# A transformer layer on one core: sums' first group prepared during the dots' last chunks, norms with few TensorE products

## The reference

```python
h = rms_norm(x, norm1_w) * (1 + sc1) + sh1
mix, ... = token_mixer(h, ...)       # attention, SSM
#   in it: y = rms_norm(y.reshape(b, L, SSM_GROUPS, gsz), ...)      2 groups
#          merged = sigmoid(ga) * (o_attn @ w_br_attn) + sigmoid(gs) * (y @ w_br_ssm)
#          mix = merged @ w_out
x = x + g1 * mix
h = rms_norm(x, norm2_w) * (1 + sc2) + sh2
x = x + g2 * peer(h, ...)
y = rms_norm(x, norm_f_w)
# peer: 16384 experts, 8 heads, top 16 of each
act = gelu(einsum('thkd,td->thk', peer_u[e], xb))
out = einsum('thk,thkd->td', g * act, peer_v[e])
```

## Time and profile before

| | us |
|---|---|
| median of 3 runs (lowest to highest) | 4533.72 (4526.81 to 4534.49) |
| time of the profiled execution | 4537.59 |
| its span | 4535.9 |
| busy PE | 4253.7 (94%) |
| busy DVE | 3162.1 (70%) |
| busy ACT | 1418.8 (31%) |
| busy POOL | 983.3 (22%) |

### The profile page before, as it was taken

How to read it: one execution, slowest core, us unless ns; L and a number is a source line. 1 busy time by engine, 2 the same in 40 slices (tenths; PEclk the granted TensorE clock), 3 DMA queues, 4 the chain that set the end, 5 groups by cost and what they waited for, 6 DMA issues and landing times. The chain is left out here.

```text
span 4535.9 us, 67898 instructions
## 1 busy us (share of the span) xinstructions
PE 4253.7 (94%) x24256; PEld 2498.9 (55%) x24256; DVE 3162.1 (70%) x5616; ACT 1418.8 (31%) x1943; POOL 983.3 (22%) x1020
## 2 busy tenths in 40 slices
PE   6999997999988899799999999999969999999997
PEld 3665663444455566466555556655635555555554
DVE  4347335455586534555889888988868888988985
ACT  3333421333321112321334444444432222222221
POOL 0000013322200001100142222222234333333320
PEclk8999998999997899999999999999989999999998
DMA  6752766555354677644586777677789888888881
GB/s 226 242 196 102 237 212 213 150 149 151 117 161 134 243 243 261 226 135 139 179 283 246 277 263 286 253 268 275 269 296 339 290 303 288 303 296 289 304 281 40
DMA packets 422568, 1039.54 MB, mean 229 GB/s; under 512 B 38498, under 2 KB 209122, under 8 KB 413730
## 3 DMA queue, kind: packets, MB, share of 16 engines
q0 software_dynamic: 112896, 396.43, 27.1%
q1 hardware_dynamic: 251970, 403.51, 25.7%
q10 hardware_dynamic: 57440, 236.35, 13.7%
HBM read 809.88 MB, written 226.27 MB: 228 GB/s over the span
## 5 line engine op out<-in xcount | busy, mean ns | idle before, releaser
L455 PE MATMUL dot_ps<-h_parts,u_parts 128*128 128x416 f16 x6144 | 1117.0, 340 | 6.8 <-issue 6.8
L455 PE MATMUL totals_ps<-act_parts,v_parts 128*128 128x416 f16 x6144 | 1083.2, 339 | 42.3 <-DVE act_parts L3219 42.3
L455 PEld LDWEIGHTS totals_ps<-act_parts,v_parts 128*128 128x128 f16 x6144 | 601.6, 98 | 522.6 <-issue 44.8
L455 PEld LDWEIGHTS dot_ps<-h_parts,u_parts 128*128 128x128 f16 x6144 | 594.9, 98 | 461.7 <-issue 14.4
L468 PE MATMUL in_ps<-h_parts_in,in_parts 128*128 128x384 f16 (+1 forms) x3168 | 515.6, 319 | 4.5 <-DVE in_parts L826 4.5
L3294 POOL DMA_INDIRECT rows_in<-in_v,row_v x204 | 302.8, 1484 | 497.7 <-DVE h L3238 484.9
L468 PEld LDWEIGHTS in_ps<-h_parts_in,in_parts 128*128 128x128 f16 x3168 | 311.0, 98 | 171.2 <-DVE in_parts L826 4.6
L2572 POOL DMA_INDIRECT u_rows_in<-tmp_u_rows,row_u x192 | 251.0, 1307 | 586.5 <-DVE row_dot L2914 558.3
L3158 ACT ACTIVATE v_parts<-v_group,units 128x1024 f16<-128x1024 f32 x128 | 136.9, 1138 | 766.8 <-PE totals_ps L455 738.1
L2674 ACT ACTIVATE gelu<-dot_ps,units 128x416 f32<-128x416 f32 x256 | 155.6, 608 | 629.4 <-PE dot_ps L455 614.9
L3230 DVE SCALAR_TENSOR_TENSOR h<-totals_ps,sum_unit,h 128x416 f32<-128x416 f32 x388 | 247.9, 647 | 139.9 <-PE totals_ps L455 139.3
(11 more groups left out here) (402 smaller groups left out, 5899.4 us busy)
## 6 DMA issues: line engine op xcount, KB each, us to landing
u_chunks<-in_u SPq DMA_DIRECT2D x128, 512.0 KB, 6.2
v_group<-in_v SPq DMA_DIRECT2D x31, 2048.0 KB, 8.3
tmp_g<-gelu ACTq DMA_DIRECT2D x128, 416.0 KB, 5.3
tmp_w<-h ACTq DMA_DIRECT2D x26, 2048.0 KB, 10.3
w_groups<-tmp_w SPq DMA_DIRECT2D x32, 1664.0 KB, 11.6
gelu_in<-tmp_g SPq DMA_DIRECT2D x31, 1664.0 KB, 7.5
tmp_u_rows<-proj_rows ACTq DMA_DIRECT2D x64, 512.0 KB, 5.4
attend_v_sweep<-in_v ACTq DMA_DIRECT2D x64, 512.0 KB, 4.3
```

What stands on the lines that cost most here:

```text
L455: mm = pe.matmul(bank, left(x), right(y), start=first and x == 0 and y == 0, stop=last and x == 1)
```

## The change

It has five parts. (1) `Norm`: DVE adds the squares of all chunks to one, and PE multiplies only that with the ones matrix, three products a norm. (2) Merge phase: the group norms' products stand behind the first branch step's 12 products with o; norm2's squares and additions stand inside the mix steps, whose loops on ACT and DVE are written out. (3) Dots phase: weight products and one-hots of the last eight chunks are earlier, 14 rows are moved out of them (2 to the first 16 chunks, 2 to each of the six turns), and in the last chunks SP loads, and ACT, DVE split, the first group of v, w and gelu, into buffers that the dots give up (the second half of the score buffer, one-hot, candidate and u buffers). (4) Sums phase: it starts with group 1's loads; the first group is only counted as done, behind the clearing of the accumulator. (5) The last norm becomes part of the sums phase: DVE gates 832 columns a chunk after each result of the last group and the 256 others in one piece (`gated_rows`), ACT squares, POOL adds chunks 0 to 4 and PE multiplies that sum and chunks 5 to 7 (12 products).

```diff
+    def add(self, dve, k):
+        dve.wait_ge(self.squared, k + 1)
+        if k > 1:
+            dve.wait_ge(self.added, k - 1)
+        total = self.sq[:, 0, :]
+        dve.tensor_tensor(total, total, self.sq[:, k, :], ALU.add).then_inc(self.added, 1)
...
         ones = self.s["const"][:, C_ONE:C_ONE + P]
-        for k in range(self.chunks):
-            pe.wait_ge(self.squared, k + 1)
-            for i, (t0, n) in enumerate(SPLITS):
-                mm = pe.matmul(self.psum[:, i, 0:n], ones, self.sq[:, k, t0:t0 + n],
-                               start=(k == 0), stop=(k == self.chunks - 1))
-                if k == self.chunks - 1:
-                    mm.then_inc(self.summed, 1)
+        pe.wait_ge(self.added, self.chunks - 1)
+        for i, (t0, n) in enumerate(SPLITS):
+            pe.matmul(self.psum[:, i, 0:n], ones, self.sq[:, 0, t0:t0 + n], start=True,
+                      stop=True).then_inc(self.summed, 1)
     def vector(self, dve):
+        for k in range(1, self.chunks):
+            self.add(dve, k)
+        self.means(dve)
...
-                group[0].tensor(pe)
-                group[1].tensor(pe)
+                def branch(i, u, norms=False):
+                    pe.wait_ge(br_in[u], (i + 1) * 64)
...
+                        pe.wait_ge(banks_taken, i * (2 * NS) + u * NS + j + 1)
+                        for k in range(NA):
+                            pe.matmul(ps[:, j, 0:n], wa[:, u, k, :], o[:, k, t0:t0 + n],
+                                      start=(k == 0), stop=(k == NA - 1))
+                        if not norms or j < 2:
+                            turn_fill(i * 2 + u, j)
+                    if norms:
+                        group[0].tensor(pe)
+                        pe.wait_ge(group[0].meaned, NS)
+                        group[1].tensor(pe)
+                        turn_fill(0, 2)
+                    if u == 0:
+                        pe.wait_ge(y_ready, KC)
...
+                for m in range(KC):
+                    for at in range(PASS * Turned.FILLS):
+                        to_rows.scalar(act, KC + m, PASS, at // Turned.FILLS, at % Turned.FILLS, SWEPT)
+                        if m > 0 and at == 4:
+                            act.wait_ge(mix_taken, m + 2)
+                            norm.square(act, m - 1)
...
+                    if m > 1:
+                        norm.add(dve, m - 1)
...
             slot = x * ND + q
-            return [n for n in range(WG // 2) if 4 + n * 11 // (WG // 2) == slot]
+            return [n for n in range(WG // 2) if 3 + n * 9 // (WG // 2) == slot]
...
-        ONEHOT_LAST = {1: 0, 2: 1, 3: 2, 5: 3}
+        ONEHOT_LAST = {1: 0, 2: 1, 3: 2, 4: 3}
         DENSE = TILES - 1
-        ROWS_FIRST = (3, 2, 2, 2, 2, 2, 3, 3, 2, 3, 3, 3, 3, 3, 3, 3)
-        ROWS_TURN = (3, 1, 2, 1, 1, 2, 2, 3, 1, 3, 2, 2, 1, 1, 3, 3)
-        ROWS_TAIL = (4, 3, 3, 3, 4, 3, 4, 4)
+        ROWS_FIRST = (3, 2, 2, 2, 2, 3, 3, 3, 3, 3, 3, 3, 3, 3, 3, 3)
+        ROWS_TURN = (3, 1, 2, 1, 2, 2, 2, 3, 1, 3, 2, 2, 2, 1, 3, 3)
+        ROWS_TAIL = (4, 3, 3, 2, 1, 1, 0, 0)
...
+                sp.wait_ge(picked, BLOCKS + DENSE)
+                for r in range(2):
+                    sp.wait_ge(w_out[r], 16 * (EARLY // 2 + 1))
+                load_w(0, EARLY)
+                for j in range(GRP):
+                    sp.wait_ge(u_split, GROUP_AT + j + 1)
+                    sp.dma_start(group["v"][:, j, :], a["v"][0, :, j, :]).then_inc(v_in[j], 16)
+                sp.wait_ge(w_done, 8 + (DENSE - 1) * WG + WG // 2)
+                for r in range(2):
+                    sp.wait_ge(g_out[r], 16 * GRP // 2)
+                sp.dma_start(group["g"], a["g"][0:GRP].rearrange("e p t -> p e t")).then_inc(g_in, 16)
+                for r in range(2):
+                    sp.wait_ge(w_out[r], 16 * (NTB // 2 + 1))
+                load_w(EARLY, NTB)
...
+                    act.wait_ge(v_in[j], 16)
+                    if j < GRP - 1:
+                        act.wait_ge(dot_done, (GROUP_AT + j + 1) * ND)
+                    else:
+                        act.wait_ge(picked, BLOCKS + DENSE)
...
+                        if x == TAIL - 1 and q == 0:
+                            for j in range(GRP):
+                                lead_a(j)
...
+                    if x == TAIL - 1:
+                        lead_v(2)
                     gelu(at, beside)
...
+                    if x == TAIL - 3:
+                        lead_v(0)
+                    if x == TAIL - 2:
+                        lead_v(1)
+                        lead_v(GRP - 1)
+                        act.wait_ge(row_dotted, NROWS)
...
+                def weigh(j):
+                    if j == 0:
+                        dve.wait_ge(g_in, 16)
+                        dve.wait_ge(w_in, 32)
+                    x = group["w"][:, :, j, :]
+                    dve.tensor_tensor(x, x, by_block(group["g"][:, j, :]), ALU.mult).then_inc(weighed, 1)
...
+                rest_v(0, 0)
+                rest_v(1, 1)
+                rest_v(2, GRP - 1)
+                for j in range(GRP):
+                    weigh(j)
+                rest_v(3, 2)
+                for j in range(GRP):
+                    rest_a(j)
...
-                load_w(0, 0)
-                for j in range(GRP):
-                    sp.dma_start(v[:, 0, j, :], a["v"][0, :, j, :]).then_inc(first_in[j], 16)
-                    sp.dma_start(gl[:, j, :], a["g"][j]).then_inc(first_in[j], 16)
+                sp.sem_inc(w_in[0], 16)
                 load_w(1, 1)
                 load_v(1, 1)
...
+                pe.wait_ge(back_taken, BACKS)
+                pe.wait_ge(held_taken, NS)
+                ones = s["const"][:, C_ONE:C_ONE + P]
+                for k in (0, *range(BY_POOL + 1, KC)):
+                    if k == 0:
+                        pe.wait_ge(norm.added, BY_POOL)
+                    else:
+                        pe.wait_ge(norm.squared, k + 1)
+                    for i, (t0, n) in enumerate(SPLITS):
...
+                for k in range(KC):
+                    if k < ROWS_GATED:
+                        act.wait_ge(rows_gated, 1)
+                    act.wait_ge(dense_gated, k + 1)
+                    if 2 < k < KC - 1:
+                        act.wait_ge(norm.added, k - 2)
+                    act.activation(square_of(k), acc[:, k, :], ACT.Square).then_inc(norm.squared, 1)
...
+                    to = acc[:, k, 0:TD]
+                    dve.scalar_tensor_tensor(to, to, s["mod"][:, 5 * KC + k, 0:1], x_of(k)[:, 0:TD], ALU.mult,
+                                             ALU.add).then_inc(dense_gated, 1)
...
+                    for k in range(KC):
+                        to = acc[:, k, TD:SEQ]
+                        dve.scalar_tensor_tensor(to, to, s["mod"][:, 5 * KC + k, 0:1], x_of(k)[:, TD:SEQ],
+                                                 ALU.mult, ALU.add)
+                    link.wait(link.base + link.n)
...
                 link.link(dve.memset(acc[:, :, :], 0.0))
                 dve.sem_inc(row_added, 1)
...
+                for done in (weighed, v_split, a_split):
+                    dve.sem_inc(done, GRP)
...
+                total = square_of(0)
+                for k in range(1, BY_POOL + 1):
+                    pool.wait_ge(norm.squared, k + 1)
+                    if k > 1:
+                        pool.wait_ge(norm.added, k - 1)
+                    pool.tensor_tensor(total, total, square_of(k), ALU.add).then_inc(norm.added, 1)
```

More of the change, by code:

```diff
@@ L232, in __init__, with square @@
         self.scaled = sem(name + "_scaled")
+    def square(self, act, k):
+        act.activation(self.sq[:, k, :], self.src[:, k, :], ACT.Square).then_inc(self.squared, 1)
     def squares(self, act, loaded=None):
@@ L237, in squares @@
                 act.wait_ge(loaded[k * 2 // self.chunks], 16 * self.chunks // 2)
[L238 removed]
+            self.square(act, k)
     def scalar(self, act, loaded=None):
@@ L2096, in _ @@
+                        branch(i, u)
                 pe.wait_ge(br_taken, KC * NS)
@@ L2496, in dots_phase, with by_block @@
         const, units = s["const"], s["units"]
+        group = s["first"]
+        EARLY = NTB - P // 2 // TB
+        GROUP_AT = NK - GRP
+        v_in = [sem(f"first_v_in{j}") for j in range(GRP)]
+        w_in, g_in = sem("first_w_in"), sem("first_g_in")
+        v_hi, v_split, weighed, a_hi, a_split = (
+            sem("first_v_hi"), sem("first_v_split"), sem("first_weighed"), sem("first_a_hi"), sem("first_a_split"))
+        def by_block(x):
+            return x.rearrange("p (b t) -> p b t", t=TB)
         u, u16, h16 = s["u"], s["u16"], s["h16"]
```

298 lines of the change are left out of this document (156 added, 142 removed).

## The result

The changed kernel takes 4541.85 us (median of 17 runs, 4534.44 to 4552.78), the kernel before 4534.49 in the same comparison (17 runs). The ratio is 1.0017, with a 95% interval of 1.0009 to 1.0024: 7 us slower, where the prediction had 8 us faster. The profiled execution of the changed kernel has a span of 4540.1 us against 4535.9.

A forecast was written before the change was run, and what follows sets the result against it. PE, busy 94% of the span, was taken as the bound. Terms 1 − 25 + 9 + 22 − 9 + 10 gave 8 us faster, 4533.7 − 8 = 4526 us; range 4513 to 4542.

The forecast's parts named there:

- norm2, +9: Norm after the mix steps: additions inside them cost nothing, reciprocals start sooner; 9 us faster (+8 to +11).
- Merge phase, −25: Start of merge phase: group norms' products wait behind o's products and their transfers, so y comes late; 25 us slower.
- First group, +22: Start of sums: PE starts at 3383 instead of 3404.9, first group's parts being done earlier; 22 us faster (+15 to +25).
- the dots' −1.3: End of dots: a new 4.1 us wait at the first weight product against a removed 2.8 us stop; net 1.3 us slower.
- Rows in the turns: Slower rival, dots turns: an added row's transfer stops PE, 3.5 us in every turn, 21 us in all; chance 0.10.
- Second group, −9: Sums phase: gelu lands 17 us after PE's start, PE stands 7.2 us and restarts slow; 9 us slower.
- Last norm, +10: End of kernel: DVE's first sum 13.5 us behind the last sum's end instead of 24.1; 10 us faster.
- norm1, +1: First norm: seven DVE additions and three slow products finish at 40.6 instead of 41.9; 1 us faster (0 to +3).
- The rival of DVE and POOL excluding each other: Last norm: DVE's gates of chunks 5 to 7 each hold up POOL's additions 1.0 us; total 4529; chance 0.05.

The follow-up runs named there:

- e1: Changed kernel with DVE's norm2 addition in the mix steps moved ahead of the wait for the step's products: 4531.47 us, ratio to the kernel before 0.9988.
- e2: Kernel before with one extra DVE addition of two chunks behind add_gated in each of the eight mix steps: 4551.98 us, ratio to the kernel before 1.0040.
- e3: Changed kernel with the group norms' products ahead of the o products again, DVE's six additions first: 4516.8 us, ratio to the kernel before 0.9962.
- e9: Kernel before with only the changed kernel's tables of single rows, 14 rows leaving the last eight chunks: 4529.71 us, ratio to the kernel before 0.9981.
- e6: Changed kernel, last norm with eight tiles for squares, POOL adding two squares to the first, PE multiplying six chunks: 4532.59 us, ratio to before 0.9997.
- e10: Changed kernel with norm2 addition moved, group 1 by twelve products, gelu issued first, POOL adding three squares, PE multiplying five chunks: 4488.43 us, ratio to before 0.9890.
- e5: Changed kernel with three counts told before the accumulator's clearing and second group's gelu issued ahead of w and v: 4535.24 us, ratio to before 1.0008.
- e4: Changed kernel with the counts weighed, v_split and a_split told ahead of the accumulator's clearing in the sums phase: 4543.36 us, ratio to before 1.0014.

## Why the prediction was wrong

**The step that failed** is in the term for norm2: "All squares but the last and all additions but two lie in the mix steps, where PE is the bound." It costs them at nothing, and that PE is the bound says only that PE's own work leaves no gap. I had not asked what is queued behind the addition on DVE. It is the reduction that releases POOL's load, for which PE's transposes wait half a step later. That loop had no slack: PE already waited 1.3 us in total for these loads in the kernel before. So 1.3 us of DVE work, on an engine idle for more than half of each step, made five stops of 2 us and once a slow clock: 11.1 us against the kernel before, 13.5 against e1, and e2 shows the same cause in the kernel before. Without this step the kernel would have come out at e1's 0.9988, where 0.9983 was predicted. That these lie so close is partly luck: e1's mix steps are 2.4 us shorter than the ones before, which the forecast did not have, and this stands against about 3 us less from the last norm and 2 us more in the dots.

The other steps:
- *Merge phase, −25:* 26.0, and every stage as worked out; e3 shows that the place did it. The gates landed at 1512.7, 17.8 us behind the phase's start, where the prediction's rows gave 17.8 too.
- *norm2, +9:* 9.5. The gain was there, and the mix steps ahead of it took it back.
- *First group, +22 with the dots' −1.3 in it:* 23.1 − 3.5 = 19.6. The boundary was right. The dots took 3.5 us more, not 1.3. The stop forecast at the first of the earlier weight products is there, 3.8 us at 3327.5 (4.1 predicted), with the granted clock at 0.51 from 3325.8 to 3332.4; the one of 2.8 us is gone. The dots' two other stops are 9.1 us together, 6.8 before, but 7.9 in e2 with the code of before: part of this is scatter, and no run was made on the rest.
- *Rows in the turns* (the slower rival): not so. e9 has the same tables and no longer dots. The stop of 3.5 us from which its price was taken is one of the two just named, which come with every table of rows. What the forecast missed is that the moved rows gain about 5 us at the boundary by themselves. How much of the changed kernel's 23 is theirs no run separates.
- *Second group, −9:* 9.1. DVE started on gelu 16.4 us behind PE's start (17 predicted), the stop was 6.3 us (7.2).
- *Last norm, +10:* 7.3, mis-sized. POOL's first addition started 0.6 us later than predicted. Two of its four additions took 0.6 us more than the others (see the point on DVE and POOL), so the last ended 7.5 us behind the last sum's end (5.7 predicted). And PE's clock was at the lower level for 5.5 us of its products (granted clock 0.50 from 4508.3 to 4513.8, then 1.00), a loss of 2.7 where 1.6 had been put in: DVE had its first sum 16.7 us behind the last sum's end, not 13.5.
- *norm1, +1:* the reciprocals start 0.3 us sooner (42.13 against 42.39), and PE's first product behind the phase came at 83.54 us against 83.45: nothing gained.
- *The rival of DVE and POOL excluding each other* held, at less than half its price. POOL's additions and DVE's gates (L3424, 832 columns, two inputs in SBUF) in the changed kernel:

```profile
4495.38 1.08 DVE L3424 SCALAR_TENSOR_TENSOR h<-h,mod,score_space 128x832 f32<-128x832 f32 x1
...
4497.69 2.27 DVE L3424 SCALAR_TENSOR_TENSOR h<-h,mod,rows_in 128x832 f32<-128x832 f32 x1
...
4501.42 1.77 DVE L3424 SCALAR_TENSOR_TENSOR h<-h,mod,rows_in 128x832 f32<-128x832 f32 x1
```

```profile
4496.60 2.49 POOL L3474 TENSOR_TENSOR onehot_space<-onehot_space 128x1088 f32<-128x1088 f32 x1 [87.19 <-ACT onehot_space L3350]
...
4499.23 3.08 POOL L3474 TENSOR_TENSOR onehot_space<-onehot_space 128x1088 f32<-128x1088 f32 x1
...
4502.46 3.07 POOL L3474 TENSOR_TENSOR onehot_space<-onehot_space 128x1088 f32<-128x1088 f32 x1
...
4505.67 2.47 POOL L3474 TENSOR_TENSOR onehot_space<-onehot_space 128x1088 f32<-128x1088 f32 x1
```

A gate takes 1.08 us when POOL is idle, as the first six of the eight do. The last two start inside an addition and take 2.27 and 1.77 us, and each ends 0.9 us behind that addition's end. The second and third addition start inside a gate and take 3.08 and 3.07 us instead of 2.49 and 2.47, and each ends 2.3 us behind that gate's end. So the one that starts second gets on only when the first is done. It cost POOL's chain 1.2 us, where the forecast's rival had 3. DVE's other operation there (L3385, one input in PSUM) took 0.64 us beside an addition and 0.65 without one. The Trainium skill's exclusive lock ("SBUF — State Buffer", two separate sides) says this, and the trace agrees. Its figure in "GPSIMD Engine Reference" (Elementwise — side-by-side cycle accounting: 4497 ns for 2048 columns, an estimate of 2.4 us here) is close to the two undisturbed additions, 2.49 and 2.47. Its advice to leave additions to VectorE (Engine selection) was not tried: e6 and e10 move some of POOL's to PE, and the end came sooner.

## What to carry to other kernels

Idle time of an engine says that it can take more work, not where. Before something is put into its list, follow what stands behind it: which buffer that frees, whose load waits for the buffer, and who waits for the load. The same additions cost 11 us or more behind `add_gated`, and nothing ahead of the wait for the products, where DVE stands idle anyway. A product moved behind others inherits their waits, here a transfer of 16 us that had been hidden. And where several loads are issued together, telling one of them earlier helps only if it also stands ahead in the queue that issues it; then the next one is late. Last, when POOL and DVE both have operations with two inputs in SBUF, count each as waiting for the other: here a gate of 1.08 us became 2.27.

## What the runs showed of the hardware

- A short stop of PE can be followed by the lower clock, and mostly is not. Of the five stops of 2.0 to 2.3 us in the changed kernel's mix steps, the first (2.07 us) had the granted clock at 0.50 for 3.4 us behind it, and four instructions took 2.74 us where the run has 1.46; behind the four others it stayed at 1.00. In e2 it was one of seven stops.
- Operations of DVE and of POOL with two inputs in SBUF did not run at the same time: gates of 1.08 us took 2.27 and 1.77 beside POOL's additions, additions of 2.49 us took 3.08 and 3.07 beside gates. Every run in which POOL adds has the same pattern (additions of 2.5 and 3.1 us, the last two gates 2.3 and 1.8).
- SP's loads that were in flight together landed in the order of their issue, and the later ones late. With five gathers of rows beside them, gelu (1.7 MB) landed 9.0 us after its issue in e5, where it goes first, and 20.5 us after in e4, with two loads ahead; w (1.7 MB) 20.4 us after in e5 with one ahead, v (2.0 MB) 24.8 us after in e5.
- SP's issue of v took 5.2 us in e4, with one load ahead in its queue, and 14.7 in e5 with two; the next load in SP's list went out only then.
- The start of the merge phase, with unchanged code ahead, scattered over 9 us between executions (1492.9 to 1501.5 in kernels with the code of before).
